# Pair-wise front slots, two heads at a time in both attentions, and two more expert chunks beside the ring

## What is computed

```python
def first_block(x, mem, ...):
    h = _rms_norm(x, norm_mix_g)
    proj = h @ w_in                     # 512 columns for pooling, 3 x 512 for q, k, v of 8 heads of 64
    attn = _moba_attention(rope(norm(q)), rope(norm(k)), v)      # causal over 256 tokens
    x = x + concat([pool, attn]) @ w_out
    x = x + _cross_attention(_rms_norm(x), _rms_norm(mem), ...)  # 4 heads of 256
    x = x + _conv_ffn(_rms_norm(x), w_up, conv_w, conv_b, w_down)  # width 2816
...
    hx, hc = modulate(x, ...), modulate(ctx, ...)
    qx, kx, vx = mla_project(...)       # 6 heads: 128 columns without and 64 with rotation
    att_x = attend(qx, k_all, v_all)    # 512 keys: 256 of x, 256 of the context
    x = x + g1 * rms_norm(concat([att_x, four_x]) @ w_out)
    yx = moe(modulate(x, ...), ...)     # 32 experts, 4 of them for each token, width 1024
    x = x + g2 * rms_norm(yx)
```

## Time and profile before

| | us |
|---|---|
| median of 3 runs | 1614.91 |
| lowest and highest run | 1614.48, 1618.3 |
| the profiled execution's own time | 1612.96 |
| its span | 1611.1 |
| TensorE busy (7234 matmuls) | 1546.0 |
| VectorE, ScalarE busy | 407.1, 301.7 |
| granted clock of TensorE, mean | 0.996 |
| moved by DMA | 513.34 MB, mean 319 GB/s |

### The profile page before, as it was taken

One profiled execution on the slowest core, in us unless ns is written; L12 is line 12 of the kernel. 1 busy time (PEld: TensorE's weight loads), 2 busy tenths in 40 slices (PEclk: granted clock), 3 DMA queues, 4 the chain that ended last, 5 costly groups with the idle time before them and its releaser, 6 DMA issues.

```text
span 1611.1 us, 18676 instructions
## 1 busy us (share of the span) xinstructions
PE 1546.0 (96%) x7234; PEld 851.3 (53%) x7234; DVE 407.1 (25%) x865; ACT 301.7 (19%) x618; POOL 9.1 (1%) x19
## 2 busy tenths in 40 slices
PE   9999999999999999999999999899999999998997
PEld 8666767888888756533333333324433333332332
DVE  1564244222223224431212121111112121111112
ACT  2223131111112234310111011111101110110111
POOL 0000000000000000000000000000000000000000
PEclk9999999999999999999999999999999999999999
DMA  9623675744443120699999999999989999999996
GB/s 389 247 105 128 283 320 190 280 157 157 150 144 123 53 105 24 280 428 428 423 428 428 429 429 428 429 428 427 418 362 426 430 429 428 428 429 428 428 428 272
DMA packets 44897, 513.34 MB, mean 319 GB/s; under 512 B 5120, under 2 KB 5264, under 8 KB 7088
## 3 DMA queue, kind: packets, MB, share of 16 engines
q1 hardware_dynamic: 43632, 507.69, 76.2%
q0 software_dynamic: 1216, 4.96, 0.9%
HBM read 511.58 MB, written 1.06 MB: 318 GB/s over the span
## 4 chain that ended last, share of the span: by engine, by line
PE 74%; DMA 20%; DVE 3%; ACT 2%; issue 1%; DVEq 0%; ACTq 0%; SPq 0%
PE bank L1165 26%; PE bank L615 12%; DMA ring<-in_gate_w 9%; PE bank L864 9%; DMA ring<-in_up_w 8%; PE bank L873 5%; DMA ring<-in_down_w 3%; PE bank L1257 3%; PE bank L1137 2%; PE bank L1197 2%; PE bank L1032 2%; PE bank L724 2%; PE bank L1182 1%; PE bank L653 1%; PE bank L680 1%; DVE squares L1865 1%
## 5 line engine op out<-in xcount | busy, mean ns | idle before, releaser
L1165 PE MATMUL bank<-ring,probs_slab 128*64 128x512 f32 x2928 | 660.6, 598 | 33.3 <-DMA ring<-in_gate_w 12.7
L1165 PEld LDWEIGHTS bank<-ring,probs_slab 128*64 128x64 f32 x2928 | 200.7, 137 | 424.4 <-issue 380.8
L864 PE MATMUL bank<-normed,ring 128*128 128x256 f32 x704 | 153.7, 379 | 0.0
L864 PEld LDWEIGHTS bank<-normed,ring 128*128 128x128 f32 x704 | 133.7, 190 | 19.0 <-issue 0.8
L2210 DVE TENSOR_TENSOR normed<-bank,big_slab 128x512 f32<-128x512 f32 x31 | 21.4, 692 | 430.7 <-PE bank L1182 430.7
L615 PE MATMUL bank<-normed,ring 128*128 128x256 f32 x448 | 98.5, 380 | 0.8 <-ACT normed L1393 0.8
L615 PEld LDWEIGHTS bank<-normed,ring 128*128 128x128 f32 x448 | 84.2, 190 | 15.1 <-issue 2.8
L2000 DVE SCALAR_TENSOR_TENSOR big_slab<-bank,par,big_slab 128x255 f32<-128x255 f32 x88 | 42.4, 482 | 166.3 <-ACT big_slab L1527 158.7
L873 PE MATMUL bank<-big_slab,ring 128*128 128x256 f32 x352 | 77.6, 379 | 0.0
L873 PEld LDWEIGHTS bank<-big_slab,ring 128*128 128x128 f32 x352 | 66.9, 190 | 9.1
L1197 PE MATMUL bank<-squares,mixed_slab 64*128 64x512 f32 x248 | 61.6, 615 | 6.3 <-ACT squares L1678 6.3
(11 more groups left out here) (332 smaller groups left out, 1179.7 us busy)
## 6 DMA issues: line engine op xcount, KB each, us to landing
ring<-in_up_w SPq DMA_DIRECT2D x63, 2048.0 KB, 22.1
ring<-in_down_w SPq DMA_DIRECT2D x63, 2048.0 KB, 22.2
ring<-in_gate_w SPq DMA_DIRECT2D x62, 2048.0 KB, 22.1
ring<-in_front_w SPq DMA_DIRECT2D x97, 1024.0 KB, 6.3
ring<-in_down_w SPq DMA_DIRECT2D x2, 1024.0 KB, 25.1
residual<-in_x SPq DMA_DIRECT2D x4, 256.0 KB, 6.5
memory_slab<-in_mem SPq DMA_DIRECT2D x1, 1024.0 KB, 16.4
context_slab<-in_ctx POOLq DMA_DIRECT2D x1, 1024.0 KB, 9.4
```

The costliest lines, as they stand in the source:

```text
L864: mm = pe.matmul(bank[bank_at][:, half * T:(half + 1) * T], w[:, (half * DC + k) * P:(half * DC + k + 1) * P], H[:, k, :], start=(k == 0), ...
L1165: mm = pe.matmul(to[half * SLOTS:(half + 1) * SLOTS, :], tokens(k), weights[:, i * D + half * HALF:i * D + (half + 1) * HALF], start=(k == ...
```

## The change

Five edits.

1. The front's ring is turned by one slot: chunk n of the front goes to slot (n + `FRONT_SLOT`) % 12, with `FRONT_SLOT` = 1. The semaphores keep n % 12.
2. In the first attention `scores` and `attend` issue two heads side by side.
3. In the second attention `latent_scores(h, t)` does heads h and h + 1 at one token half: two matmuls over 128 rows, then two over 64 rows in the two halves of the array. `KR_of` and its three VectorE steps are gone. The order of products, of exponentials, of maxima and of normalisations changes with it.
4. Chunks 200 and 201, the first two gate chunks of place 17, go into the slabs that chunks 47 and 49 have used (`late_slab`), once chunk 49 has been used. The ring's positions after them move up by two.
5. The loops of SP are split so that places 17 and 18 are written out, and the counts of the ring follow.

```diff
+FRONT_SLOT = (FIRST_SLOT - FRONT) % RING
...
-                sp.dma_start(ring[:, n % RING, :], front_w[n]).then_inc(chunk_here[n % RING], 16)
+                sp.dma_start(ring[:, (n + FRONT_SLOT) % RING, :], front_w[n]).then_inc(chunk_here[n % RING], 16)
...
             def front_in(slot):
-                return STREAM[FRONT - 1 - (FRONT - 1 - slot) % RING]
+                return STREAM[FRONT - 1 - (FRONT - 1 + FRONT_SLOT - slot) % RING]
...
-    + ["a00", "a01"]
-    + [n for h in range(LHEADS) for n in
-       ([f"a{h + 1}0", f"a{h + 1}1"] if h + 1 < LHEADS else []) + [f"at{h}0", f"at{h}1"]
-       + ([f"ao{h - 1}"] if h else [])]
+    + ["a00", "a10", "a01", "a11"]
+    + [n for h in range(0, LHEADS, 2) for n in
+       [name for t in range(2) for name in
+        [f"at{h}{t}", f"at{h + 1}{t}"]
+        + ([f"a{h + 2}{t}", f"a{h + 3}{t}"] if h + 2 < LHEADS else [])]
+       + [f"ao{h}"] + ([f"ao{h + 1}"] if h + 2 < LHEADS else [])]
...
+                        if at in LATE:
+                            sp.wait_ge(s_chunk, STASHED.stop)
+                            for c in range(2):
+                                load_one(late_slab[c], w, e, 2 * p + c, late_here[c])
+                        else:
+                            pair_at(at, w, e, p)
...
+            def scores(j):
+
+                if j == 0:
                     pe.wait_ge(s_rot, 4)
+                to = [begin(f"s{2 * j + i}") for i in range(2)]
+                q, k = [[QK[HEAD * i:HEAD * (i + 1), at, :] for i in range(2)] for at in (j, 4 + j)]
+                for i in range(2):
+                    pe.matmul(to[i][:, 0:P], q[i][:, 0:P], k[i][:, 0:P], start=True, stop=True)
+                for i in range(2):
+                    end(pe.matmul(to[i][:, P:P + T], q[i][:, P:T], k[i], start=True, stop=True))
...
+                for tokens, keys, at, first, last in ((0, 0, 0, True, True), (P, 0, P, True, False),
+                                                      (P, 1, T, False, True)):
+                    for i in range(2):
+                        h = 2 * j + i
+                        mm = pe.matmul(o[HEAD * i:HEAD * (i + 1), tokens:tokens + P],
+                                       V1[:, keys, h * HEAD:(h + 1) * HEAD], PTu[:, h % 4, at:at + P],
+                                       start=first, stop=last)
                 end(mm)
...
             def latent_scores(h, t):
-                o = begin(f"a{h}{t}")
-                pe.matmul(o[:, :], QN[:, h, t * P:(t + 1) * P], KN[:, h, :], start=True, stop=False)
-                end(pe.matmul(o[:, :], QR[:, h // 2, t * P:(t + 1) * P], KR_of[h % 2],
-                              start=False, stop=True))
+
+                at = slice(t * P, (t + 1) * P)
+                to = [begin(f"a{h + i}{t}") for i in range(2)]
+                for i in range(2):
+                    pe.matmul(to[i][:, :], QN[:, h + i, at], KN[:, h + i, :], start=True, stop=False)
+                for i in range(2):
+                    of = slice(ROPE * i, ROPE * (i + 1))
+                    end(pe.matmul(to[i][:, :], QR[of, h // 2, at], KR[of, :], start=False, stop=True))
...
-            latent_softmax(0, "max")
-            for h in range(LHEADS):
-                latent_softmax(h, "normalise")
-                if h + 1 < LHEADS:
-                    latent_softmax(h + 1, "max")
+            latent_max(0, 0)
+            latent_max(0, 1)
+            for h in range(0, LHEADS, 2):
+                for t in range(2):
+                    for i in range(2):
+                        read(dve, f"a{h + i}{t}")
+                        normalise(((0, 2 * T),), HEADS + XHEADS + 2 * h + 2 * t + i, 2 * t + i)
+                    if h + 2 < LHEADS:
+                        latent_max(h + 2, t)
```

More of the change, by code:

```diff
@@ L54, with ring_turn @@
 FIRST_SLOT = 2
-LAST_CHUNK = EXPERT_CHUNKS - 1 - STASH
-assert STASH % 2 == 0 and STASHED.start % 2 == 0
+AFTER_DOUBLE = 2 * PART + DOUBLE * ITEM_CHUNKS
+LATE = range(AFTER_DOUBLE, AFTER_DOUBLE + 2)
+BESIDE = STASH + len(LATE)
+LAST_CHUNK = EXPERT_CHUNKS - 1 - BESIDE
+assert STASH % 2 == 0 and STASHED.start % 2 == 0 and len(LATE) % 2 == 0
 assert RING == ITEM_CHUNKS and DOUBLE % 2 == 0 and STATIC < DOUBLE and STATIC % 2
+def ring_turn(at):
+    if at < STASHED.start:
+        return at
+    return at - (STASH if at < LATE.start else BESIDE)
 def expert_at(place):
@@ L292, in build_program @@
         stash_here = [sem(f"stash_here{i}") for i in range(STASH)]
+        late_here = [sem(f"late_here{i}") for i in range(len(LATE))]
         s_in = {n: sem(f"loaded_{n}") for n in
@@ L475, in front_in @@
             def front_in(slot):
-                return STREAM[FRONT - 1 - (FRONT - 1 - slot) % RING]
+                return STREAM[FRONT - 1 - (FRONT - 1 + FRONT_SLOT - slot) % RING]
+            in_turn = [at for at in range(EXPERT_CHUNKS) if at not in STASHED and at not in LATE]
             def pair_at(at, w, e, p):
-                r = at if at < STASHED.start else at - STASH
+                r = ring_turn(at)
                 if r < RING:
@@ L483, in pair_at @@
                 else:
-                    freed = r - RING if r - RING < STASHED.start else at - RING
-                    sp.wait_ge(s_chunk, freed + 2)
+                    sp.wait_ge(s_chunk, in_turn[r - RING] + 2)
                 load_pair(w, e, p, r)
@@ L604, in tile @@
                     opened.add(c)
[L605 removed]
+                return ring[:, (c + FRONT_SLOT) % RING, t * P:(t + width) * P]
             def project(name, first, k_chunks, moving, m_chunks=2, width=T, ready=None):
@@ L749, in attend @@
                 read(pe, f"t{2 * j}")
[L750 to L758 removed]
+                for tokens, keys, at, first, last in ((0, 0, 0, True, True), (P, 0, P, True, False),
[5 more added lines that the diff above has]
+                                       start=first, stop=last)
                 end(mm)
[L762 to L763 removed]
+            for j in range(2):
+                scores(j)
             cross_values(0, 0)
@@ L767, in _ @@
                 turn_probs(h)
-            for h in range(4, 8):
-                scores(h)
+            for j in range(2, 4):
+                scores(j)
             cross_values(1, 0)
@@ L856, in ff_up @@
                     pe.wait_ge(s_ff_conv, f - 3)
-                return ring[:, slot, :]
+                return ring[:, (slot + FRONT_SLOT) % RING, :]
             def ff_up_matmuls(bank_at, w, ready=lambda k: None):
@@ L894, in ff_pair @@
                 pe.wait_ge(s_ff_act, 2 * s)
-                ff_down_matmuls((k - 1) % 2, ring[:, slot, :], first)
+                ff_down_matmuls((k - 1) % 2, ring[:, (slot + FRONT_SLOT) % RING, :], first)
             pe.wait_ge(s_mod_read, MOD_ROUNDS)
@@ L905, in _ @@
             pe.wait_ge(s_ff_act, FF_CHUNKS)
-            ff_down_matmuls(0, ring[:, slot, :], False)
+            ff_down_matmuls(0, ring[:, (slot + FRONT_SLOT) % RING, :], False)
             in2 = FIRST_CHUNK["in2"] * TILES
@@ L1158, in expert_product @@
                         weights = stash[at - STASHED.start]
-                    else:
-                        weights = in_ring(at - (0 if turns is None and at < STASHED.start else STASH),
-                                          0 if turns is None else turns * 16)
+                    elif turns is None and at in LATE:
+                        pe.wait_ge(late_here[at - LATE.start], 16)
+                        weights = late_slab[at - LATE.start]
+                    elif turns is None:
+                        weights = in_ring(ring_turn(at))
+                    else:
+                        weights = in_ring(at, turns * 16)
                     for i in range(2):
@@ L1252, in wide_product @@
                 for c in range(PART):
-                    weights = in_ring(first + c - STASH)
+                    weights = in_ring(ring_turn(first + c))
                     for i in range(2):
```

139 lines of the change are left out of this document (61 added, 78 removed).

## The result

The changed kernel took 1626.94 us (median of 6 runs, 1624.22 to 1630.98), the kernel before 1615.26 us beside it: ratio 1.0076, 95% interval 1.0066 to 1.0086. It is slower by 0.7 to 0.9%, 11.7 us by the medians. The forecast was 1618.7 with a range up to 1623; the direction was the forecast's, the size was three times too small. The profiled execution took 1625.24 us (1612.96 before), its span is 1623.4 us (1611.1).

A forecast was written before the change was run, and what follows sets the result against it. TensorE's timeline was taken to bound everything before the experts, then TensorE and DMA by turns. Terms -0.5 + 0 - 0.35 + 4.3 + 0.3 = +3.75 us gave 1616.7 profiled, 1618.7 us median; own range 1616 to 1621, with rivals 1612 to 1623.

The forecast's parts named there:

- What bounds: Whole kernel: TensorE's timeline ahead of the experts sets later starts; 31.0 us of waits for expert weights stay.
- Edit 1, -0.5: Front slots: loads start earlier, but at most 0.8 us of the 8.7 us debt carries past 796 us; -0.5 us.
- edit 4, 0: Two late chunks: the extra room is gone once place 17 uses them; 0 us, bounds 0 and -1.1.
- Edit 2, -0.35: First attention: scores two heads side by side end earlier; -0.35 us, bounds 0 and -1.
- 0.2 earlier: First attention: the last two scores, side by side from 129.15 us, take 0.64 us and end 0.2 earlier.
- Edit 3, the gaps, +8.3: Second attention: TensorE waits bare for the softmax three times, at at00, at01 and at21, 2.76 us each; +8.3 us.
- 0.43 apart: Second attention: two scores of a pair end 0.43 us apart, used in working out the 2.5 us gap.
- Edit 3, packing, -4.6: Second attention: two 64-row matmuls together take 0.96 us, not 1.72; six pairs save 4.6 us.
- The clock, a rival at 0.10: Second attention: gaps of 2.5 us might drop TensorE's clock to 1.2 GHz; 1622 us; chance 0.10.
- Many waits near 1 us did not do it: Second attention: argument against the falling clock, that many waits near 1 us had not lowered it.
- Contention, +0.3: At ao5: two slab loads beside the router's tables delay the last table; +0.3 us, bounds 0 and +1.1.
- two slabs last only 4.9 us: At ao5: reason for taking +0.3 us where a table landing 3.7 us later would cost 0.7.

The follow-up runs named there:

- e2: The kernel before with only the front's ring slots turned by one; 1615.14 us, ratio 0.9996.
- e4: The kernel before with only the two late chunks put into spent slabs and SP's loops split to match; 1615.66 us, ratio 1.0001.
- e7: The changed kernel, order kept, with the rotated key at 128 rows with zeros again, so no 64-row matmuls side by side; 1624.35 us, ratio 1.0061.
- e8: The kernel before with both attentions packed and the second reordered, outputs between the two halves' scores; old slots, no late chunks; 1615.61 us, ratio 1.0001.
- e5: The changed kernel with ten matmuls of ones ahead of each of the three waits at turns in the second attention; 1622.34 us, ratio 1.0043.
- e1: The kernel before with only the second attention's change; 1626.42 us, ratio 1.0064.
- e6: The changed kernel with VectorE taking both halves' maxima before both halves' normalising in the second attention; 1624.47 us, ratio 1.0053.
- e10: The changed kernel with the last two first-expert slabs released later, by the mixing projection's first product; 1622.98 us, ratio 1.0045.
- e3: The changed kernel with the second attention's change undone; 1614.95 us, ratio 0.9995.
- e9: e8 with the rotated key at 128 rows with zeros, so no 64-row matmuls side by side in the second attention; 1616.24 us, ratio 1.0003.
- e11: The changed kernel with e8's order of the second attention and e10's later slab release; 1613.91 us, ratio 0.9995.
- e12: The changed kernel with the second attention undone as in e3 and e10's later slab release; 1614.49 us, ratio 0.9997.

## Why the prediction was wrong, step by step

- *What bounds.* Right: 31.0 us of waits for weights before and after, and everything behind the attention moved as a block.
- *Edit 1, -0.5, and edit 4, 0.* Not contradicted: e2 and e4 can't be told from 0, and -0.5 is too small to be seen. The mechanism is as said: debt gone at 694, lead gone by 808.
- *Edit 2, -0.35.* The sum is right, -0.3, and its parts are not. "0.2 earlier" for the last scores failed: the products behind the two groups of scores are 17.78 us apart (113.35 to 131.13) where they were 17.69. Two heads side by side need two free banks, and TensorE now stands idle for 0.53 us ahead of 129.23, until ScalarE's copy frees the second. From 131.13 to the next projection it is 19.61 us instead of 20.11: the product with the values, which I had taken as running together already, gained (1.47 us from 145.06 to 146.53, before 1.73), and made up for it.
- *Edit 3, the gaps, +8.3.* Right in place and number, a little small in size: 2.67, 2.93 and 2.67 us of waiting where 2.5 was worked out, and 0.34 more each, where 0.28 was, as the second of two turns waits for its own normalising (1.22 us from 605.78 to 607.00, usually 0.88). That is 3.1 per gap and 9.3 in all. What failed in the working is "0.43 apart": the two scores end together, and the maximum starts 0.16 us behind their end (603.21), where 0.27 - 0.43 had it 0.16 ahead. ao4 waited 0.7, not 0.9.
- *Edit 3, packing, -4.6.* Mis-sized: a pair takes 1.06 us, not 0.96, and the four records ahead of it take 1.88 instead of 1.72, together 2.94 instead of 3.44 us: 0.5 per pair, 3.0 in all. The rule of the Trainium skill (TensorEngine Tiling (Array Packing), Key Properties) that a change of tiling mode drains TensorE pointed this way. I had weighed it at 0.5 us in all; by these rows it was 1.6. And e7 shows what the sum could not: this term and the gaps weren't independent. Without packing the gaps would have been 2.9 us shorter. Added up with measured sizes, gaps and packing give the right total, yet packing's own worth is some 0.5 us (0.4 in e8's order), not 3.
- *The clock, a rival at 0.10, should have been a term.* The sum had it at nothing. It cost 2.7 us of the profiled stretch (e5). "Many waits near 1 us did not do it" was no evidence about gaps of 2.7, of which the old trace had none in this stretch. The rival said that it decides as soon as one stage falls; two fell.
- *Contention, +0.3.* The price of a table beside slabs was taken from the down-bias table as 3.7 us more; it was 4.8, and the wait 1.7 us. I cut it to 0.3 because "two slabs last only 4.9 us", but the tables are in the queues in just these 5 us. The upper bound of 1.1 was too low as well.

Sum with the measured terms: second attention -3.0 + 9.3 + 0.7 - 0.3 + 2.7 = 9.4 (the trace has 9.7), slots 0, first attention -0.3, tables 1.7: 10.8 us against 11.7 by the medians. The rest, 0.9 us, stays open; single runs of the kernel before differ by more (1612.2 to 1618.4). The steps that failed, with the error of each: the clock, left out of the sum (2.7), packing's size (4.6 taken, 3.0 measured: 1.6), the tables (0.3 taken, 1.7 measured: 1.4) and the length of the gaps (8.3 taken, 9.3 measured: 1.0); all four erred to the same side.

## What to carry to other kernels

Before two heads, tiles or units are put side by side on TensorE, follow the whole chain to the next instruction that needs them: if the engines between (here a maximum, an exponential and a normalising per unit) pace that chain, the saved matmul time becomes waiting, and the order of independent work between producer and consumer decides. Two results computed side by side are ready together, so the engine that takes them one by one starts later against their end than when they come one after the other. A bare gap of some 2 to 3 us on a busy TensorE should be costed with the stage at half clock that may follow it. Small table loads that are needed within a few microseconds should not be asked for in the same moment as megabyte loads.

## What was not expected of the hardware

- Gaps of 1.8 to 2.9 us between dense matmuls were often followed by a stage at a granted clock of about half, some 3.4 us long (0.93 over the 49.3 us of the changed kernel is 6.9 us at half for two stages). Of three such gaps it followed two in the changed kernel, in e1 three, in e6 two, in e7 and e10 one; with the gaps filled to 0.5 us (e5) none. The kernels without such gaps (before, e2, e3, e4, e8, e9, e11, e12) had none in this stretch.
- A part of the front that no edit touches loses 1.7 us to such a stage near 235 us in some profiles (changed kernel, e1, e2, e6, e7, e8) and not in the other eight: this view of windows is of the changed kernel, where before has 1.00.

```profile
234.00:240.00 6.00, 5.13 (x16) 4.26 (x17) 1.14 (x5) 1.89 (x5) 0.00 (x0) 0.72 0.99 410
```

- Float32 matmuls of 64 rows in the two halves of the array: 4 records in 1.06 us between matmuls of 128 rows, where 8 took 1.91 in the combine; and the 128-row records ahead of them run 0.09 to 0.20 us longer as a group of four.
- A table of 16 KB landed after 7.8 us when asked for beside two 1 MB loads on another queue, and after 3.0 us alone.
